# Hybrid decoder layer: weight sums with a buffer of their own, and the work of first tiles and part 0 in another order

## The reference

```python
def swiglu(x, w1, w3, w2):
    return (jax.nn.silu(x @ w1) * (x @ w3)) @ w2

def block(x, ...):
    x = x + 0.5 * rmsnorm(swiglu(rmsnorm(x, norm_g[0]), ffn1_w1, ffn1_w3, ffn1_w2), norm_g[1])
    mo, st = mixer(rmsnorm(x, norm_g[2]), ...)
    x = x + rmsnorm(mo, norm_g[3])
    x = x + 0.5 * rmsnorm(swiglu(rmsnorm(x, norm_g[4]), ffn2_w1, ffn2_w3, ffn2_w2), norm_g[5])
    return x, st
```

## Time and profile before

| | |
|---|---|
| median of 3 runs | 1102.76 us (1102.58 to 1103.33) |
| profiled execution | 1100.35 us, of which the span of the trace is 1098.5 us |
| TensorE busy | 1056.8 us (96%) |
| VectorE, ACT, GpSimd busy | 652.5, 411.9, 161.8 us |
| granted TensorE clock, mean | 0.993 of full speed |

### The profile page before, as it was taken

How to read it: one execution, slowest core, us unless ns; L and a number is a source line. 1 busy time by engine, 2 the same in 40 slices (tenths; PEclk the granted TensorE clock), 3 DMA queues, 4 the chain that set the end, 5 groups by cost and what they waited for, 6 DMA issues and landing times. The chain is left out here.

```text
span 1098.5 us, 21180 instructions
## 1 busy us (share of the span) xinstructions
PE 1056.8 (96%) x8729; PEld 1040.3 (95%) x8729; DVE 652.5 (59%) x1072; ACT 411.9 (37%) x650; POOL 161.8 (15%) x209
## 2 busy tenths in 40 slices
PE   8999999999999999999999999968999989999998
PEld 7999999999999999998999999968999989999997
DVE  6534433433333379784577778756883588368746
ACT  6322124222122345321447544433552255234432
POOL 0000716910000000520000000041320122022100
PEclk9999999999999999999999999979999999999999
DMA  7222322223222240223411152221323133312222
GB/s 255 78 95 77 96 77 96 82 90 92 81 77 95 72 140 22 75 78 119 138 59 58 40 175 88 96 67 49 115 93 111 30 116 123 94 41 91 82 73 82
DMA packets 31509, 99.40 MB, mean 90 GB/s; under 512 B 3780, under 2 KB 6212, under 8 KB 31304
## 3 DMA queue, kind: packets, MB, share of 16 engines
q1 hardware_dynamic: 31432, 98.33, 27.7%
HBM read 93.58 MB, written 4.74 MB: 89 GB/s over the span
## 5 line engine op out<-in xcount | busy, mean ns | idle before, releaser
L1304 DVE TENSOR_TENSOR wl<-raw,wh 128x1024 fp32r<-128x1024 f32 (+2 forms) x117 | 135.6, 1159 | 264.3 <-ACT wh L705 263.6
L705 ACT CAST wh<-raw 128x1024 fp32r<-128x1024 f32 (+2 forms) x117 | 114.3, 978 | 312.2 <-PE ps L2489 250.4
L2489 PE MATMUL ps<-xh,wh 128*128 128x272 f32 x1040 | 218.4, 291 | 13.1 <-DVE wl L1304 12.0
L2489 PE MATMUL ps<-xl,wh 128*128 128x272 f32 x1040 | 216.1, 289 | 0.0
L2489 PE MATMUL ps<-xh,wl 128*128 128x272 f32 x1040 | 215.6, 289 | 0.0
L2489 PEld LDWEIGHTS ps<-xh,wh 128*128 128x128 f32 x1040 | 164.1, 190 | 14.6 <-DVE wl L1304 12.9
L2489 PEld LDWEIGHTS ps<-xl,wh 128*128 128x128 f32 x1040 | 164.9, 190 | 0.0
L2489 PEld LDWEIGHTS ps<-xh,wl 128*128 128x128 f32 x1040 | 163.8, 190 | 0.0
L2720 PE MATMUL ps<-hh,wh 128*128 128x272 f32 x304 | 63.4, 290 | 7.1 <-DVE wl L1304 7.0
L2489 PE MATMUL ps<-hh,wh 128*128 128x272 f32 x304 | 63.2, 289 | 0.3 <-DVE hl L1325 0.3
L2720 PE MATMUL ps<-hl,wh 128*128 128x272 f32 x304 | 62.8, 288 | 0.0
(11 more groups left out here) (572 smaller groups left out, 2421.5 us busy)
## 6 DMA issues: line engine op xcount, KB each, us to landing
raw<-w SPq DMA_DIRECT2D x66, 512.0 KB, 3.6
pair<-w SPq DMA_DIRECT2D x36, 512.0 KB, 4.5
raw<-win SPq DMA_DIRECT2D x25, 512.0 KB, 3.7
raw<-w SPq DMA_DIRECT2D x32, 384.0 KB, 3.2
raw<-wout SPq DMA_DIRECT2D x8, 512.0 KB, 4.0
raw<-w SPq DMA_DIRECT2D x12, 256.0 KB, 2.7
o_yT<-x SPq DMA_DIRECT2D x8, 272.0 KB, 2.2
cs<-cT SPq DMA_DIRECT2D x4, 516.0 KB, 4.7
```

The source lines that it names most:

```text
L705: nc.scalar.copy(wh[par][:, 0:cols], raw[par][:, 0:cols]).then_inc(hi_done, 1)
L1304: V.tensor_tensor(wl[par][:, 0:cols], raw[par][:, 0:cols], wh[par][:, 0:cols].bitcast(F32), ALU.subtract).then_inc(split_done, 1)
L2489: last = mm(ps[:, bank + s, 0:HALF], w[:, kk * P:(kk + 1) * P], a[:, kk, s * HALF:(s + 1) * HALF], start=(kk == 0 and i == 0), stop=(kk == ...
```

## The change

- `sums` moves from the memory of raw to the unused fourth quarter of the base operands (over xh and xl), as [128, 2, ...].
- SP: a part's down loads 0 and 1 are issued behind its first pair load, without waits for sums; in part 0, load_pair(1) goes behind down loads 0 and 1. A pair load also waits for g_lo.
- The first tile of each part: sum_13, hi_3/lo_3, hi_a22/lo_a22 and hi_4/lo_4 move among the down units before it (in part 0 too).
- In the tile loop, VectorE: c11 ahead of lo_4, c22 ahead of lo_g, lo_a22(j) from ahead of c11 to behind lo_3(j+1). ACT: hi_a22(j) from ahead of silu_pair to behind hi_g(j+1).
- In part 0: unit 6's lo ahead of the xn operations, unit 7's split ahead of the forms; bases and forms spread among the down units, the fourth form last; the down units' evacuation by ACT (`down_copy`) instead of VectorE.
- TensorE, end of parts 1 to 3: down unit 0 is finished after two tiles of down unit 1 instead of five.

```diff
-        sums = sb("sums", [P, 4 * KHP], at=raw_at)
+        sums = sb("sums", [P, 2, KD * T], at=xh_at + 12 * FORM)
...
@@ SP, load_pair @@
                     spe.wait_ge(a22_lo, j - 1)
+                    spe.wait_ge(g_lo, j - 1)
                     spe.wait_ge(s4_sum, j - 1)
@@ SP, ffn2 @@
-                load_pair(1)
...
+                    for j in range(N6 * (p - 1), N6 * p) if p else ():
+                        if j + 2 < NG:
+                            load_pair(j + 2)
+                        if j % N6 == 0:
+                            down(0)
+                            down(1)
+                    if p == 0:
                         down(0)
-                        spe.wait_ge(s4_lo, last + 1)
                         down(1)
-                        if last + 2 < NG:
-                            load_pair(last + 2)
-                    for m in range(2 if p else 0, KD):
+                        load_pair(1)
+                    for m in range(2, KD):
                         down(m)
@@ ACT @@
+            def down_copy(m):
+                act.wait_ge(unit_used, down_unit(0, m) + 3)
+                act.wait_ge(form_lo, (4, 4, 5, 5, 7, 7, 7, 7)[m])
+                nc.scalar.copy(halves(y[:, m, :]), pair(down_set(0) + 2 * (m % 2))).then_inc(y_evac, 1)
...
                 up_split(u0 + 6)
+                up_split(u0 + 7)
                 silu(hb + 2, 0)
                 hi_form(0, form_hi_t[:, 2], form_t3[:], 1.0)
-                hi_form(1, ...)
-                hi_form(2, ...)
-                hi_form(3, ...)
-                up_split(u0 + 7)
                 hidden_hi(hb + 2, 0, 2)
...
                         down(0)
+                        hi_form(1, form_hi_t[:, 0], xn[:, 0, 1], 1.0)
                         silu(hb + 3, 1)
+                        hi_form(2, form_hi_t[:, 1], form_t24[:], -1.0)
                         down(1)
+                        hi_base(0, xn[:, 0, 0])
                         hidden_hi(hb + 3, 1, 3)
+                        down(2)
+                        down_copy(0)
+                        hi_base(1, xn[:, 1, 0])
+                        down(3)
+                        down_copy(1)
+                        hi_base(2, xn[:, 1, 1])
+                        down(4)
+                        down_copy(2)
+                        hi_form(6, form_hi_t[:, 3], form_t24[:], 1.0)
+                        down(5)
+                        down_copy(3)
+                        hi_3(0)
+                        hi_a22(0)
+                        down(6)
+                        hi_4(0)
+                        down_copy(4)
+                        down(7)
+                        down_copy(5)
+                        hi_g(0)
+                        down_copy(6)
+                        hi_12(0)
+                        down_copy(7)
...
+                        if j > j0:
                             hi_4(j)
-                            hi_a22(j)
+                            silu_pair(j - 1)
+                        keep_p1(j)
...
+                            hi_g(j + 1)
+                        if j > j0:
+                            hi_a22(j)
@@ VectorE @@
+                up_lo(u0 + 6)
                 for kk in range(KD):
                     normed(kk)
-                up_lo(u0 + 6)
                 up_first(hb + 2, 0, u0 + 4)
-                lo_form(0, ...)
-                lo_form(1, ...)
-                lo_form(2, ...)
+                up_lo(u0 + 7)
                 scaled(hb + 2, 0)
-                lo_form(3, ...)
-                up_lo(u0 + 7)
                 gated(hb + 2, 0, u0 + 5)
                 hidden_lo(hb + 2, 0, 2)
...
                         down(0)
+                        lo_form(0, form_lo_t[2][:], form_t3[:], form_hi_t[:, 2], 1.0)
                         up_first(hb + 3, 1, u0 + 6)
                         scaled(hb + 3, 1)
+                        lo_form(1, ...)
                         gated(hb + 3, 1, u0 + 7)
+                        lo_form(2, ...)
                         down(1)
                         hidden_lo(hb + 3, 1, 3)
+                        lo_form(3, ...)
+                        down(2)
+                        lo_form(4, ...)
+                        down(3)
+                        lo_form(5, ...)
+                        down(4)
+                        sum_13(0)
+                        lo_form(6, ...)
+                        down(5)
+                        lo_3(0)
+                        lo_a22(0)
+                        down(6)
+                        lo_4(0)
+                        down(7)
+                        lo_g(0)
+                        lo_12(0)
...
+                        if not last:
+                            sum_13(j + 1)
+                        if j > j0:
+                            c12(j - 1)
+                        c11(j)
+                        if j > j0:
                             lo_4(j)
+                            c22(j - 1)
+                        if last:
+                            down(0)
+                        else:
+                            lo_g(j + 1)
+                            lo_3(j + 1)
+                        if j > j0:
                             lo_a22(j)
+                        if last:
+                            down(1)
+                        else:
+                            lo_12(j + 1)
+                        if j > j0:
+                            hidden(j - 1)
+                            hidden_lo(FT4 + j - 1, 0, j - 1 - j0)
...
+                        sum_13(N6 * p)
+                        down(2)
+                        evac(0)
+                        lo_3(N6 * p)
+                        lo_a22(N6 * p)
+                        down(3)
+                        evac(1)
+                        lo_4(N6 * p)
@@ TensorE @@
                         down(0, range(3, n - 1))
                         enter_down(1)
-                        down(1, range(0, n - 1))
+                        down(1, range(0, 2))
                         down(0, range(n - 1, n))
-                        down(1, range(n - 1, n))
+                        down(1, range(2, n))
```

More of the change, by code:

```diff
@@ L308, in build @@
         N6 = PARTS2[1]
-        S2B, S4B, S1B, S3B = (slice(i * KHP, (i + 1) * KHP) for i in range(4))
+        s2_raw, s4_raw, s1_raw, s3_raw = (sums[:, b, i * KHP:(i + 1) * KHP] for b in range(2) for i in range(2))
         A21B, A22B, A11B, A12B = (slice(i * KHP, (i + 1) * KHP) for i in range(4))
@@ L904, in ffn2 @@
[L904 to L908, removed]
-                            hi_4(j)
-                            hi_a22(j)
[L911 to L930, removed]
@@ L933, in ffn2 @@
+                    silu_pair(j)
+                    hidden_hi(FT4 + j, 0, N6 - 1)
+                    if p < len(PARTS2) - 1:
+                        down(2)
+                        hi_3(N6 * p)
+                        hi_a22(N6 * p)
+                        down(3)
+                        hi_4(N6 * p)
+                        for m in range(4, KD):
                             down(m)
-                        hi_3(N6 * p)
                         hi_g(N6 * p)
@@ L1420, in lo_3 @@
             def lo_3(j):
-                low(s3_hi, j, s3_w[j % 2][1][:], sums[:, S3B], s3_w[j % 2][0][:], s3_lo)
+                low(s3_hi, j, s3_w[j % 2][1][:], s3_raw, s3_w[j % 2][0][:], s3_lo)
             def lo_a22(j):
@@ L1428, in lo_4 @@
             def lo_4(j):
-                low(s4_hi, j, s4_w[1][:], sums[:, S4B], s4_w[0][:], s4_lo)
+                low(s4_hi, j, s4_w[1][:], s4_raw, s4_w[0][:], s4_lo)
             def c11(j):
@@ L1525, in ffn2 @@
-                        dve.wait_ge(form_lo, 7)
-                    else:
-                        j0 = N6 * (p - 1)
-                        for j in range(j0, j0 + N6):
-                            last = j == j0 + N6 - 1
-                            if not last:
-                                sum_13(j + 1)
-                            if j > j0:
-                                c12(j - 1)
-                            lo_4(j)
-                            lo_a22(j)
-                            c11(j)
-                            if last:
-                                down(0)
-                            else:
-                                lo_g(j + 1)
-                            if j > j0:
-                                c22(j - 1)
-                            if last:
-                                down(1)
-                            else:
-                                lo_3(j + 1)
-                                lo_12(j + 1)
-                            if j > j0:
-                                hidden(j - 1)
-                                hidden_lo(FT4 + j - 1, 0, j - 1 - j0)
-                        c12(j)
-                        c22(j)
-                        hidden(j)
-                        hidden_lo(FT4 + j, 0, N6 - 1)
@@ new lines, in ffn2 @@
+                    c12(j)
+                    c22(j)
+                    hidden(j)
```

(11 more changed lines are left out.)

76 lines of the change are left out of this document (43 added, 33 removed).

## The result

The changed kernel takes 1089.86 us (median of 4 runs, 1089.51 to 1090.08); the kernel before took 1102.67 beside it (1102.52 to 1103.33). The ratio is 0.9882, with a 95% interval of 0.9865 to 0.9899. The forecast was 1091.5 with a range of 1084 to 1101.5. The profiled execution of the changed kernel has a span of 1087.7 us.

A forecast was written before the change was run, and what follows sets the result against it. TensorE bounds the kernel, busy 1056.8 of 1098.5 us, so only its idle and low-clock time can be won. Gains of 8.7 us (part 0) and 2.6 us (parts 1 to 3) take 1102.8 to 1091.5 us, range 1084 to 1101.5.

The forecast's parts named there:

- Part 0: Part 0 and the two up units before it: reordered queues cut lost time from 19.2 to 10.5 us, gain 8.7.
- The evacuation at no cost: Part 0's down units: the eight evacuations, moved to ACT, cost nothing; the closest split is 0.4 us early.
- Parts 1 to 3, what goes: Tile loop and down units of parts 1 to 3: waits for third down units, c22 and g_lo go, 17.9 us.
- Parts 1 to 3, what comes: Tile loop: later lo_a22 delays the pair's transfer, so TensorE waits 5.1 us a part, 15.3 in three; net gain 2.6.
- the ring: Tile loop: from keep_p1 through lo_a22, transfer and sum back to keep_p1 takes 12.35 us, 1.8 over 10.6.
- the sign to look for: Tile loop: VectorE idle ahead of sums, ended by the pair's DMA, 2 to 4 us nine times.
- 1 (the transfer isn't late): Tile loop: transfer lands in under 3 us or lo_a22 goes first; 15.3 us not lost, 1076 us; chance 0.10.
- 3 (transfers of 6.1): Tile loop: transfers of 6.1 us cost 9 x 1.05 us more; 1101 us, no change; chance 0.06.
- 2: Part 0: hidden_lo(hb+3) gets the turn before GpSimd's fourth form, 2.4 us less; 1089 us; chance 0.08.
- 4 (the clock stays low in the tile loop): Tile loop: TensorE's clock stays low, eating the gain or, over whole tiles, making 1170 us; chance 0.05.
- The sum: Whole kernel: -8.7 and -2.6 make -11.3 us; profiled execution 1089.1, median 1091.5 us.
- the forecast's first step: From 700 us on: 30.8 us in 16 TensorE waits, two for up-unit splits (12.0), 14 for weight splits and sums.

The follow-up runs named there:

- the second profile: The changed kernel measured a second time, unedited: 1090.3 us, ratio 0.9899 to the kernel before.
- experiment 3: The changed kernel, with GpSimd's fourth form in part 0 waiting until hidden_lo(hb+3) is done: 1087.95 us.
- experiment 6: The changed kernel with another order in part 0: up_first(hb+3) ahead of hidden_lo(hb+2), hidden_lo(hb+3) ahead of down(1), ACT following suit: 1087.61 us.
- experiment 4: The kernel before, with only TensorE's order of the down units at the ends of parts 1 to 3 changed: 1094.84 us.
- Experiment 1: The changed kernel, with hi_a22(j) back ahead of silu_pair on ACT and lo_a22(j) ahead of c11 on VectorE: 1072.87 us.
- experiment 2: The changed kernel, with load_pair(j) of most tiles also waiting for lo_12(j-1), a later step in the tile: 1115.07 us.
- experiments 7 to 9: Changed kernel with both orders (edits of experiments 1 and 6); then down loads 2, 3 ahead of load_pair(1); then fourth form later: 1070.56, 1070.42, 1068.56 us.
- Experiment 9: The e8_pair1_last kernel, with VectorE's down(2) and down(3) splits earlier in part 0 and GpSimd's fourth form behind down(3): 1068.56 us.
- e7_again: Second run of the changed kernel with the edits of experiment 1 and experiment 6 together: 1068.68 us, ratio 0.9688.
- e8_pair1_last: The e7_again kernel, with SP's loads of part 0's down units 2 and 3 ahead of load_pair(1): 1070.42 us, and 1069.54 when run again.

## Why the prediction was right

**Part 0.** Forecast: 19.2 us lost become 10.5. Unit 7 was to start at 718.3 and began at 719.2, after a wait of 0.3 (forecast 0.5); the whole trace is 1.0 us late already when unit 5 ends, where the change has done nothing yet (in the profiles of the kernels that share the code up to there, unit 7 starts anywhere from 717.5 to 720.2), so on TensorE's scale of before it is 718.2. The wait ahead of the first down unit is 2.34 (2.4). The wait inside it was to be 5.8 and is 3.87, or 5.3 in the second profile. The low clock takes the difference: in the first profile the clock had fallen after the 2.34 already, so that the matmuls ahead of the long wait came 0.45 apart where 0.25 is usual, and what they lose the wait loses. TensorE stands still until hidden_lo either way. p2(0) was to be near 758.5 and is at 758.94, less the 1.0: 757.9. The gain was 9.3 us, 8.7 were forecast. The cause named, that GpSimd's fourth form has the turn ahead of hidden_lo(hb+3), is confirmed by experiment 3; that the banks of the first down unit wait for up_first(hb+3) by experiment 6, where up_first goes earlier and that wait is gone (0.3 is left, for the unit's split).

**The evacuation at no cost.** Right: no wait for it. Put back on VectorE it costs a wait of 0.8 us.

**Parts 1 to 3, what goes.** All of the earlier trace rows is gone, as forecast, and experiment 4 shows which part the order of TensorE has in it: it alone clears the third down units.

**Parts 1 to 3, what comes.** The step with the greatest risk was that lo_a22, moved behind lo_3(j+1), makes the transfer late, and the transfer TensorE. The forecast was waits of 0.9, 1.6 and 1.6 in each part. Measured in the three parts: 0.93, 1.53, 1.44; 0.83, 0.96, 1.50; 0.87, 1.01, 0.81. The first, which depends only on when lo_a22 is done and how long a transfer takes, is right within 0.1. The others are shorter on the whole, though the ring's second turn was slower than forecast (12.81 us against 12.35). VectorE idled 17.3 us ahead of the nine sums, 1.9 each and at most 2.3, where the sign to look for was 2 to 4. The nine p1 waits of 0.2 were seen only as one of 0.45 in each part's last tile. Forecast for all 15.3 us, measured 9.9 + 2.0 + 18 x 0.16 = 14.8, and 16.6 with the 0.10 behind each restart, which the forecast left out. Experiment 1 takes the ring away and the waits go; experiment 2 lengthens it and they grow. The mechanism is shown in both directions.

**The rivals.** 1 (the transfer isn't late) and 3 (transfers of 6.1) fall by VectorE's row: 5.07 us in the first turn, 5.50 in the second. 2 falls by GpSimd's row at 732.13. 4 (the clock stays low in the tile loop) falls for this change: in all windows from 740 us to 1080 the granted clock is 1.00. By the rule of the Trainium skill named in the forecast ("TensorE: Matmul & The Clock Gate", "A second HAM failure mode: psum-queue depth-cycling") the waits of 0.8 to 1.5 us would have cost the clock; the page reports this of another kernel, in bf16. The trace doesn't agree for these. For the waits of 1.5 to 3.7 us of experiment 2 it agrees in one part of three: 0.93 in the windows of part 3, 1.00 in parts 1 and 2.

**The sum.** Forecast -11.3; measured -12.8 by the medians and -10.8 by the two spans (1098.5 and 1087.7). The profiles can be cut up: part 0 gained 9.3 where 8.7 was forecast; from p2(0) to the end 331.2 became 328.8, which is 2.4 where 2.6 was forecast; and 1.0 was lost ahead of unit 6, which the change doesn't touch. So on the scale of the profiles, where the forecast was 1089.1 and 1089.51 was measured, it is off by 0.4, and each term within 0.7; that the total is closer still is luck, as the 1.0 lost ahead of unit 6 hides what part 0 gave beyond its forecast. The other 2 us are in the step from the profile to the median: the forecast added 2.4, which is how far the kernel before's profiled execution lay below its median, and the changed kernel's lies only 0.35 below. In the tile loop errors cancelled in part: the waits for keep_p1 were 9.9 us and not 12.3, there were eighteen waits to restart from and not twelve, and every restart costs more than the 0.16, before as after. One name is wrong in the forecast's first step: of the 14 smaller waits six are for c22, a partial result in PSUM, and no split or sum of weights; the sums that follow treat them rightly.

**What was left in it.** The change makes a ring through a transfer for which it gives away 16.6 us by the profiles and 17.0 by the medians. The best versions measured (experiments 7 to 9) are at 0.969 to 0.972 of the kernel before and some 1.8 to 2% below the changed kernel. Experiment 9's 1068.56 is the lowest and differs from the 1068.68 of `e7_again` by nothing that can be measured; nor do 8 and 9 show a gain over 7.

## What to carry to other kernels

Where an operation frees a buffer for a load, its place in the queue is a due time as much as that of one that feeds TensorE: follow the ring (free, transfer, first use, what is queued behind that use, back to the freeing operation) and add it up; when the sum is longer than the tile it costs the difference in each tile. Removing a wait in a stretch with several tight engines shows the next one, often at the same instruction: a load, VectorE's turn and, by the times alone, a bank held the third down unit one after the other, so price such an edit by the second latest of its inputs. Two lines that change only the order of matmuls brought, alone, over half of what the whole change did.

## What the runs showed of the hardware that was not expected

- The same idle time of TensorE lowers its clock in one execution and not in another. After 2.3 us it fell in one profile of the changed kernel and held in the other (unit 7 to p2(0): 39.7 and 40.3 us); after 3.05 us (`e8_pair1_last`) the matmuls came 0.45 us apart where 0.25 is usual, for 6 us, and after 3.07 (`e8_again`, the same kernel) the clock stayed at 1.00; in experiment 2 waits of 3.5 us left it at 1.00 in parts 1 and 2 and one of 3.7 was followed by the low level in part 3. So a profile with the clock up behind a wait doesn't show that an edit has cured it.
- A restart costs TensorE 0.16 us ahead of the first matmul and 0.10 behind it (0.07 at the waits of the kernel before). With both, the eighteen small waits of the tile loop account for all of the 16.6 us that experiment 1 takes out of it.
- The second transfer of the ring took 0.4 us longer than the first (5.50 against 5.07), and the waits of TensorE differ from part to part (1.44 and 1.50, but 0.81 in part 3) under the same program, and in the second profile are others again (1.04, 1.57, 0.96 in part 1 where the first has 0.93, 1.53, 1.44). No run tests why.
